# The second pass of a hybrid trunk projects two token blocks at a time, over two blocks

## The reference, cut to what matters

```python
u = rms_norm(x, norm_gain) * (1 + scale) + shift      # (4096, 1024)
proj = u @ w_in                                        # pool_v|pool_g|r|k|v|w_down|a_down|rg
y_pool = multiscale_pool(proj[..., :512]) * silu(proj[..., 512:1024])
p = proj[..., 1024:2688]                               # r|k|v|w_down|a_down: 13 tiles of 128 columns
p = p + (token_shift(p) - p) * mu                      # mixes each token with the one before
w_log = -softplus(-(w0 + tanh(wd) @ w_lora_up)) - 0.5;  decay = exp(-exp(w_log))
a = sigmoid(a0 + ad @ a_lora_up)
kk = l2_normalized(k * k_k);  k = k * (1 + (a - 1) * k_a)
y = wkv7_scan(r, decay, k, v, -kk, kk * a)             # S_t = S diag(w) + (S a) b^T + v k^T; y = S r
y = group_norm(y) * lnx_w + lnx_b + sum(r * k * r_k) * v
y_rwkv = y * silu(proj[..., 2688:3200])                # rg: 4 tiles of 128 columns
h = x + gate * (concat(y_pool, y_rwkv) @ w_out)
out = rms_norm(h, final_gain)
```

## Time and profile before

| | us |
|---|---|
| median of 3 runs (2818.44 to 2819.74) | 2818.65 |
| the profiled execution, its own time | 2816.01 |
| its span, first to last instruction | 2814.20 |
| PE busy | 2742.1 |
| PE weight loads busy | 2308.4 |
| DVE busy | 1513.4 |
| ACT busy | 1127.3 |
| POOL busy | 479.2 |
| L941, the projection of the second pass, PE busy | 1072.8 |
| L349, the projection of the first pass, PE busy | 449.7 |

### The profile page before, as it was taken

How to read it: one execution, slowest core, us unless ns; L and a number is a source line. 1 busy time by engine, 2 the same in 40 slices (tenths; PEclk the granted TensorE clock), 3 DMA queues, 4 the chain that set the end, 5 groups by cost and what they waited for, 6 DMA issues and landing times.

```text
span 2814.2 us, 77652 instructions
## 1 busy us (share of the span) xinstructions
PE 2742.1 (97%) x30981; PEld 2308.4 (82%) x30981; DVE 1513.4 (54%) x3455; ACT 1127.3 (40%) x2850; POOL 479.2 (17%) x627
## 2 busy tenths in 40 slices
PE   6999999999899999999999999999999999999996
PEld 6777777777778888888888888888888888888884
DVE  2411212212256766666666666666666766666664
ACT  3332333323134444444444444444444344444442
POOL 3111011110112112111111112111121121111210
PEclk8999999999999999999999999999999999999997
DMA  8623223133100000000100000000000000001000
GB/s 339 244 81 112 84 95 119 71 107 105 45 32 24 32 24 24 24 24 24 35 28 28 28 24 24 24 24 31 33 24 32 24 24 24 24 24 39 24 17 24
DMA packets 68709, 153.12 MB, mean 54 GB/s; under 512 B 3977, under 2 KB 37342, under 8 KB 66398
## 3 DMA queue, kind: packets, MB, share of 16 engines
q1 hardware_dynamic: 63134, 130.08, 13.1%
q0 software_dynamic: 1680, 11.01, 1.0%
q10 hardware_dynamic: 3632, 7.87, 0.8%
HBM read 98.61 MB, written 50.33 MB: 53 GB/s over the span
## 4 chain that ended last, share of the span: by engine, by line
PE 95%; DVE 2%; DMA 1%; ACT 1%; issue 1%; SPq 0%; ACTq 0%; DVEq 0%
PE bank L941 37%; PE bank L349 15%; PE bank L991 12%; PE bank L977 8%; PE bank L381 8%; PE bank L1118 2%; PE bank L1058 1%; PE bank L1034 1%; PE bank L1045 1%; PE bank L951 1%; PE bank L1066 1%; PE bank L1094 1%; PE bank L1067 1%; PE bank L970 1%; PE bank L958 1%; PE bank L965 1%
## 5 line engine op out<-in xcount | busy, mean ns | idle before, releaser
L941 PE MATMUL bank<-xT,w 128*128 128x128 f32 x8704 | 1072.8, 280 | 10.0 <-DMA xT<-xt_dram 10.0
L941 PEld LDWEIGHTS bank<-xT,w 128*128 128x128 f32 x8704 | 1001.8, 192 | 37.7 <-issue 11.0
L1227 ACT ACTIVATE XX<-bank 128x128 f32<-128x128 f32 x640 | 156.0, 277 | 834.1 <-PE bank L991 833.7
L349 PE MATMUL bank<-xT,w 128*128 128x256 f32 x2048 | 449.7, 382 | 4.8 <-ACT xT L469 4.8
L349 PEld LDWEIGHTS bank<-xT,w 128*128 128x128 f32 x2048 | 392.3, 192 | 65.7 <-issue 10.5
L1495 DVE STREAM_TRANSPOSE XX<-XX 128x256 f32<-128x256 f32 x256 | 112.6, 440 | 416.5 <-ACT XX L1227 416.4
L977 PE MATMUL bank<-wo,Y 128*128 128x512 f32 x512 | 232.4, 597 | 4.6 <-DVE Y L1455 4.6
L381 PE MATMUL bank<-wo,yc 128*128 128x512 f32 x512 | 224.7, 592 | 0.0
L671 DVE TENSOR_SCALAR gate<-gate 128x1024 f32<-128x1024 f32 x16 | 11.1, 694 | 368.9 <-ACT gate L489 368.9
L1330 POOL TENSOR_TENSOR LA<-SM,ones 64x256 f32<-64x256 f32 x128 | 92.7, 724 | 561.2 <-DVE Y L1455 538.6
L991 PE MATMUL bank<-XX,AI 64*64 64x64 f32 x5120 | 183.1, 220 | 5.1 <-DVE XX L1533 5.1
(11 more groups left out here) (181 smaller groups left out, 3544.1 us busy)
## 6 DMA issues: line engine op xcount, KB each, us to landing
x_in<-in_x SPq DMA_DIRECT2D x16, 1024.0 KB, 7.7
xr<-in_x SPq DMA_DIRECT2D x32, 512.0 KB, 4.3
xt_dram<-xT SPq DMA_DIRECT2D x32, 512.0 KB, 8.6
h_dram<-xr SPq DMA_DIRECT2D x32, 512.0 KB, 2.6
xT<-xt_dram SPq DMA_DIRECT2D x32, 512.0 KB, 3.3
gate_row<-h_dram SPq DMA_DIRECT2D x32, 512.0 KB, 3.3
out<-gate_row SPq DMA_DIRECT2D x32, 512.0 KB, 2.6
w<-in_w_in POOLq DMA_DIRECT2D x8, 1088.0 KB, 11.1
```

Source lines behind the costliest of these rows:

```text
L349: last = nc.tensor.matmul(bank[t // 2][:, (t % 2) * T1:(t % 2 + 1) * T1], w1[:, k, t * P:(t + 1) * P], xT[:, k, :], start=(k == 0), stop=( ...
L941: last = nc.tensor.matmul(bank[b][:, q * P:(q + 1) * P], w2[:, k, (t0 + q) * P:(t0 + q + 1) * P], xT[par][:, k, :], start=(k == 0), stop=( ...
L1227: s(nc.scalar.activation(XX[j][:, k, 2 * a:2 * a + 2].rearrange(flat), level_bank(j, a)[:, 128:256], ACT.Copy), xx_ready, hold=False)
```

## The change

The second pass now projects blocks in pairs. `xT` is one buffer of 256 tokens, a matmul of the projection has 256 moving columns in place of 128, and the two blocks ahead are projected during two blocks: the even block n issues the units of the first 9 tiles of blocks n+2 and n+3 (`SPLIT`), the odd block n+1 those of the other 8.

- `SLOTS` now has units of a quarter of a column tile: 2 matmuls of 256 tokens, 4 records. The pair has 17 x 4 = 68 units, 36 in the even and 32 in the odd block. The calls of `fill` are the same, so what changes in number is the last fill of a block.
- There are nine groups of one or two tiles. ACT writes each to `mix0` (even block) and to `mix1` or `early` (odd block), DVE adds to the same place; `prev` is gone.
- Seven mixed tiles and two gate tiles of the odd block are done before the odd block in work has been through with `mix1` and `rg`. They are staged in `early`, and POOL moves them in four operations (`stage`) at the end of the odd block. The carried column is copied by POOL in two operations early in the even block.
- `xT` has one buffer, loaded in two halves of its rows' tiles: the first when the last units no longer need it (`xT_free`), the second when the pair's projection is done.
- Blocks 30 and 31 have no projection to fill with (before: block 31 alone).
- At the meeting, SP issues the first loads of `xT` ahead of the first pass's last stores, the prologue projects blocks 0 and 1, DVE's four last residual additions are spread between the steps of block 0's head, and POOL, which now writes over the place of `xr`, waits for the last stores.
- The first pass stores `xT` with one DMA a block in place of two; the eight loads of the gate's weights share four semaphores.

```diff
-            xT = [new(f"xT2{j}", [P, KT, T2]) for j in range(2)]
-            mix = new("mix", [P, MIX, T2])
-            prev = new("prev", [P, MIX, 1 + T2])
-            rg = new("rg", [P, NP, T2])
+            xT = new("xT2", [P, KT, T1])
+            mix0 = new("mix0", [P, MIX, T2])
+            mix1 = new("mix1", [P, MIX, 1 + T2])
+            early = new("early", [P, 9, 1 + T2])
+            mix = [mix0, mix1[:, :, 0:T2]]
+            rg = new("rg", [P, NP, T1])
...
-            GROUPS = [(12, 1, 0), (0, 4, 1), (4, 4, 0), (8, 4, 1), (13, 4, 0)]
-            SLOTS = [(gr, q, k) for gr, (_, n, _) in enumerate(GROUPS) for q in range(n) for k in (0, KT // 2)]
+            GROUPS = [(12, 1, 0), (0, 2, 1), (2, 2, 0), (4, 2, 1), (13, 2, 0), (6, 2, 1), (8, 2, 0), (10, 2, 1), (15, 2, 0)]
+            AHEAD = 5
+            SLOTS = [(gr, q, k) for gr, (_, n, _) in enumerate(GROUPS) for q in range(n) for k in range(0, KT, 2)]
+            SPLIT = sum(n for _, n, _ in GROUPS[:AHEAD]) * KT // 2
+            EARLY = {12: 0, 0: 1, 1: 2, 2: 3, 3: 4, 4: 5, 5: 6, 13: 7, 14: 8}
...
-                    m = [0]
+                    more = ahead == 2
+                    m = [SPLIT if par else 0]
                     def fill(k=1):
                         for _ in range(k):
-                            if ahead and m[0] < len(SLOTS):
-                                project(m[0], n + 1, 1 - par)
+                            if more and m[0] < (len(SLOTS) if par else SPLIT):
+                                project(m[0], n - par + 2)
                                 m[0] += 1
...
-                    for k in range(k0, k0 + KT // 2):
-                        last = nc.tensor.matmul(bank[b][:, q * P:(q + 1) * P], w2[:, k, (t0 + q) * P:(t0 + q + 1) * P], xT[par][:, k, :],
+                    for k in range(k0, k0 + 2):
+                        last = nc.tensor.matmul(bank[b][:, q * T1:(q + 1) * T1], w2[:, k, (t0 + q) * P:(t0 + q + 1) * P], xT[:, k, :],
...
+                def stage():
+                    px.wait(mix_ready, shifted(3))
+                    px.wait(rg_ready, 2)
+                    moved(mix1[:, 12:13, :], 12, 1)
+                    moved(mix1[:, 0:4, :], 0, 4)
+                    moved(mix1[:, 4:6, :], 4, 2)
+                    moved(rg[:, 0:2, T2:T1], 13, 2)
...
+                    if more and par:
+                        s.wait(lhs_ready, 1)
+                        s.wait(rgate_ready, 1)
+                        stage()
                     if ahead:
                         head(n + 1)
...
                     store_xT(n)
+                    if not more:
+                        sp.wait_ge(xT_stored, 16 * N1)
+                        sp.wait_ge(proj_ps.sem, proj_ps.at(n, 4))
+                        first_loads()
                     store(n - 1)
```

More of the change, by code:

```diff
@@ L1088, in run @@
                         variance()
+                    if not par:
+                        po.wait(mix_ready, shifted(7))
+                    elif more:
+                        px.wait(mix_ready, shifted(3))
                     bonus_sum()
@@ L1098, in run @@
                     s.wait(bk_ready, 1)
-                    s.wait(rg_ready, 1)
+                    if not par:
+                        po.wait(rg_ready, 4)
+                    elif more:
+                        px.wait(rg_ready, 2)
                     if first:
@@ L1361, in run @@
                     s.wait(v_ready, 1)
+                    if first:
+                        for j in range(2):
+                            pool.wait_ge(h_stored[j], 16 * N1)
                     for t, ready in ((SV, sv_ready), (UV, uv_ready)):
@@ L1503, in run @@
                     hd.block(n + 1)
+                    px.block(n - par + 2)
+                    more = ahead == 2
                     if not first:
@@ L1538, in run @@
                         group_gate()
-                    if ahead:
-                        shift(n + 1, 0)
+                    if more and not par:
+                        shift(0)
                     level(1)
@@ L1549, in run @@
                         residual(n - 1, 0)
-                    if ahead:
-                        shift(n + 1, 1)
+                    if more and not par:
+                        shift(1)
                     level(4)
```

286 lines of the change are left out of this document (180 added, 106 removed).

## The result

| | before | after |
|---|---|---|
| median, us | 2818.55 (2816.74 to 2819.74, 4 runs) | 2834.93 (2832.69 to 2835.35, 4 runs) |
| ratio, 95% interval | | 1.0057 (1.004 to 1.0074) |
| profiled execution, its own time, us | 2816.01 | 2834.73 |
| its span, us | 2814.20 | 2833.0 |

The change makes the kernel 16 us slower, where 10 were forecast. It is the forecast's case, and its range of 2823 to 2840 holds the time.

What follows compares the result with a forecast made beforehand. PE bounds the kernel, its waits just covered by fill; -27.8 (wider records) + 28 (split) + 13.5 (meeting) - 3.6 (end) = +10.1 on 2816.0, giving a median of 2828.7 us, range over all 2802 to 2848.

Steps and rivals of the forecast that it cites:

- the forecast's case: Whole kernel: slower by 10.1 us, to 2828.7 us, own range 2823 to 2840; chance 0.5.
- What bounds the kernel: Loop blocks: PE bounds, just in time, with 0.45 us slack over a gapless ACT and DVE chain covered by fill.
- 256 columns: Projection in filled blocks: wider records make even blocks 0.8 us longer and odd 2.65 shorter, -27.8 us in all.
- The split, S: Starts of even blocks 2 to 28: shorter last fill makes PE wait 2.0 us each (0.3 to 3), +28 us.
- The meeting: Between first pass and block 1: earlier loads -11.4, longer prologue +28.3, block 0's start -3.4, sum +13.5 us.
- GpSimd: POOL's four moves in every second block: 3 us more finds room, costing 0 if DVE is not held up.
- Block 30: Now unfilled: 5.1 + 48.7 + 2.5 = 56.3 us against 63.9 before, -7.6 us.
- H: Block 30: what the head of block 31 adds there, 2.5 us (1.1 to 5).
- Block 31: Last block: its lhs 2.5 us later and 1.5 us for the lower clock, +4.0 us.
- Rival 1: Even starts: slack suffices because the chain follows PE, a wait of 0.3 us each, faster at 2799 us; chance 0.18.
- Rival 3: Every block: a further wait, 0.7 us in 29 blocks, +20, slower still at 2849 us; chance 0.12.
- rival 2: Kernel's ends cost less: block 30 at 53 us, no clock loss; no change, 2820 us; chance 0.2.

Runs made afterwards that it cites:

- experiment 2: Changed kernel with odd blocks' level fills 3, 3, 1, 2, 2 units in place of 3, 3, 3, 3, 2, so a longer last fill: 2808.62 us.
- experiment 3: Kernel before with odd blocks' last-level fill 4 units in place of 2, so a last fill shorter by two units: 2847.15 us, ratio 1.01.
- experiment 6: Changed kernel with POOL's moves done twice, three more copies at the end of every odd block: 2836.84 us, ratio 1.0061.
- experiment 1: Changed kernel with odd blocks' first fill 4 units in place of 6, so the last fill is 6 in place of 4: 2836.49 us.
- experiment 7: Changed kernel, block 30 only: low-rank matmuls of block 31's head behind the first solve, ACT's evacuation ahead of the head's exponentials: 2836.48 us.
- experiment 5: Changed kernel with the loads of xT for blocks 2 and 3 issued ahead of the first pass's last stores: 2835.78 us, ratio 1.0054.

## Why the prediction was right, and where it was not

**What bounds the kernel: right.** The slack of 0.45 us in the earlier trace rows and the two engines working without a gap in the earlier trace rows were the right view to rest on. Experiments 2 and 3 show it from both sides: with the cover given back the wait goes, with the cover taken from the kernel before it comes.

**256 columns: right.** Forecast +0.8 and -2.65 us a block. The odd blocks went from 62.78 to 60.25, -2.53, and with the wait gone (experiment 2) the pair is 1.69 shorter, 25 us over 15 pairs. The rows of this kernel, with 27.8, were near; the 10 us that the prediction worked out from the Trainium skill, "TensorE: Matmul & The Clock Gate", section "Back-to-back issue gap", are not what the trace shows.

**The split, S: right in kind, too small.** It was 2.0 a block. Measured, from the end of L1163's 0.55 us at 1562.66 to L1172 at 1564.36, are 1.70 us where I had 1.55; at the second input, 1.79 - 1.18 = 0.61 (after less experiment 2) where I had 0.45. Together 2.31. Of the 0.15 at the first, 0.1 is that LA now ends 5.12 us behind the block's start and before 3.01: PE is 2.1 us early, where I had 2.0. The other 0.05 are the time from LA's end to PE's start, which the sum had left out. Blocks 1 to 29 were off by 5.1 us: 14 x 0.31 = 4.3 by S, 14 x 0.12 = 1.7 by the odd blocks, and -0.9 by block 1. That one took 64.29 us in before, with a stall of 1.19 us in it, and 60.71 in after.

**The meeting: right, the last digit by luck.** +14.3 with block 0's own 0.8, and +14.3. The wait is gone, and from L1008 to the fill are 8.5 us, forecast 8.4; that was read off the queue of DMAs. But L381 began 0.64 us earlier in after than in before, by nothing that the change does: over nine profiled kernels of this case it begins between 714.2 and 717.6. And from the first fill to block 1 are 1.47 us more than before, not 0.8, since the fill behind the wait ran 7.13 us.

**GpSimd: right.** Its moves lie in idle time (experiment 6), as they do doubled.

**Block 30: the step that failed is the sum 5.1 + 48.7 + 2.5, which has no term for stalls.** H, the 2.5 us for the head of block 31, held. The start of the block was right: L1172 at 2700.61, 5.17 us behind L1013. From there to the tail's L1013 are 55.08 us. The prediction's base, block 31 of before, took 48.17 from L1118 on. The other 6.91 us, by steps: +0.51 up to the first L1077, where a stall of DVE (2.05 us) stands at the place of one of PE in before (2.53). +3.13 from there to L1088, of which 1.73 is a stall with no releaser and 1.40 the low-rank matmuls. +2.22 to L1101: ACT ended its exponentials 0.19 us behind the end of L1088 and then stood 2.12 us before L1295, with nothing to wait for. -0.44 and +1.49 around the second evacuation, for which ACT, with sigmoids until 2750.68, came late. The head's own part is 1.40 + 0.10 + 1.05 = 2.55 us. The two stalls behind L1077 are 3.85, and 5.17 + 48.17 + 0.51 + 2.55 + 3.85 = 60.25. Both stand on the way from step to step, so PE pays them in full.

The prediction read the 2.81 us "issue" before the second evacuation of block 31 as room for ACT. That was right, though the profile names no releaser: in all twelve profiled executions this evacuation starts 0.08 to 0.09 us behind the end of the matmuls that it reads. In before these are, ending at 2787.18, and ACT's L1234 starts at 2787.26:

```profile
2786.06 1.12 PE L1045 MATMUL bank<-R,XX 64*64 64x64 f32 x16 [0.68 <-DVE R L1476]
```

**Block 31: right in the sum**, 3.7 for 4.0, and this too in part by luck. Block 30's clock was at 0.50 from 2751 on and PE began block 31 at it. The block starts its Gram step 2.30 us later than before and the tail is 1.7 us longer, 4.0 together; but block 31 of before had a stall of 2.53 us, and after had two, of 0.33 and 0.86.

**The rivals.** Rival 1, the cover holds, is what experiment 2 made come true by another split. The sign of the change hung on where three units stand. Rival 3, a further wait in every block, did not come. The end did not cost less (rival 2) but more.

## What to carry to other kernels

When work that fills gaps is divided anew, the calls that hand it out keep their numbers and the last one takes what is left; look at what that last piece covered before counting what the new form saves. Take filler where PE has other work beside it, not from the piece in front of an engine's chain, and check the next input in line too, since a wait moved from there comes back whole. In an edit that only moves DMAs in a queue look for the cheap part of a large change: four lines at the meeting were worth 11 us. And a stretch of a trace that serves as the base of a forecast brings its own stalls along and says nothing of those of the new program: block 31 of before had 2.53 us of them in its 48.7.

## What the runs showed of the hardware that was not expected

**Stalls with nothing to wait for.** The profile's "issue" is time in which an engine waited for nothing that it shows. In the second pass of the changed kernel and its variants PE has them nearly all in the blocks that are written out (0, 1, 30, 31), 0.3 to 3.2 us each; of the 28 blocks of the loop three of the profiled executions have one such stall (1.25 to 1.53 us, in front of the last record of an L1034), the others none. They lie at fixed places in the program: in all of them the first L1077 of block 30 is cut into 13 and 3 records, with 0.98 to 1.73 us between, and the first L1088 of block 31 into 6 and 10, with 0.86 to 1.42. One place comes and goes, in front of the last 4 records of an L1034 of block 30: none in after and in experiments 1 and 7, 2.45 to 3.22 us in the others. They sum to 4.0 us in after and 12.1 in experiment 2. ACT has one too in block 30, 2.10 to 2.29 us in the changed kernel and its variants, and DVE one of 2.05 to 2.23.

The time behind a stall is dear as well. In experiment 5 the stall of 3.22 us in block 30 is followed by an L1020 of 6.53 us, where after has 3.70; the granted clock there was 0.50. Together that is 6.1 us, and the block was 5.6 longer. So block 30, where it was not edited, took 60.25, 65.86 and 63.91 us in three kernels (after, experiments 5 and 6). Runs of one kernel spread over 3 to 12 us. That this has the same cause is likely and not shown, for one execution of each was profiled. An effect of 3 us at one place is read from its rows and can't be read from the median.

What the engines waited for can be told from the DMA records. The profile has two queues that it calls "instruction": q8, in pieces of 16,384 bytes, and q14, of 8,192. In after, for the window of the stall before L1077 (2732.8 to 2735.0), the view of the DMAs has one transfer:

```profile
q8 instruction: 1, 0.02, 2.8%
```

It ended at 2733.82, and PE went on at 2735.01, 1.19 us later. It is so everywhere. In the twelve profiled executions PE has 53 stalls of this kind of 0.25 us and more behind 740 us, and each of them ends 1.19 to 1.55 us behind the end of such a transfer of q8. ACT's 12 (the waits of 2.81 us are not of this kind, see above) and DVE's 12 end 1.14 to 1.38 us behind one of q14. Of random moments about 5% lie 1.1 to 1.6 us behind a transfer of q8. So these are waits for the engine's own instructions, as far as coincidence in time can show it; no run moved them on purpose. The Trainium skill, "Runtime: NRT & Kernel Launch", section "Instruction fetch mechanics", says that engines fetch their instructions in blocks of 16 KiB by a DMA queue of their own, mostly hidden. The trace agrees on the pieces of q8, and on "mostly": in the loop's blocks of after 181 such transfers cost PE nothing. In the blocks that are written out some cost up to 3.2 us, on the path. Why those are not hidden stays open.

**DVE and GpSimd.** The final norm has two inputs in SBUF and took 1.75 us beside POOL's copies and 1.28 without them. One by one (experiment 6): POOL's copy of 516 columns was running when DVE's operation began, and kept its 1.04 us, to 1668.91. The next copy, of 258 columns, began at 1668.99 and took 1.48 us in place of 0.62, until 0.47 us behind the end of DVE's operation at 1670.00. That is how it would look if each of the two, once it has its turn, keeps the other out until it ends. The prediction took this from the Trainium skill, "SBUF — State Buffer", section "Who interferes with whom". The page says of two SBUF inputs that they contend, calls the shared ports "an exclusive lock", and has "fully blocks" in its line on DVE's 2-port modes. The rows agree with a lock held for one instruction, and not with one held for POOL's whole series. In block 0 the same happens to t (L1546), 1.64 us against 0.69 in the loop, beside a POOL operation of the head (L1423).
